# Latent attention on one core: rotary scores of the last three head pairs as two rounded passes over stacked query and residue, with the rotary projection copied to SBUF by ScalarE

## What is computed

```
q = (cq @ w_uq).reshape(B, S, 8, 128 + 64)
q_rope = apply_rope(q[..., 128:], cos, sin)
k_rope = apply_rope(d[..., 512:576], cos, sin)
s = (q_nope . k_nope + q_rope . k_rope) * sm_scale
p = softmax(where(key_pos <= q_pos, s, -inf))
o = p @ v
apply_rope: x1 * cos - x2 * sin, x2 * cos + x1 * sin
```

## Time and profile before

| | before |
|---|---|
| median of 3 runs (lowest, highest) | 1292.56 us (1291.3, 1292.88) |
| profiled execution, its time | 1291.86 us |
| profiled execution, its span | 1290.1 us |
| granted TensorE clock over the span | 0.999 |
| PE busy | 98% of the span |
| DVE busy | 72% |
| ACT busy | 47% |
| score steps of the latent attention | from 420.45 us to about 505.5 us |

### The profile page before, as it was taken

One profiled execution on the slowest core, in us unless ns is written; L12 is line 12 of the kernel. 1 busy time (PEld: TensorE's weight loads), 2 busy tenths in 40 slices (PEclk: granted clock), 3 DMA queues, 4 the chain that ended last, 5 costly groups with the idle time before them and its releaser, 6 DMA issues.

```text
span 1290.1 us, 19557 instructions
## 1 busy us (share of the span) xinstructions
PE 1268.9 (98%) x7451; PEld 1111.2 (86%) x7451; DVE 924.1 (72%) x1224; ACT 608.9 (47%) x888; POOL 31.4 (2%) x29
## 2 busy tenths in 40 slices
PE   8999999999999999999999999999999999999997
PEld 7799999988888777888999998888888878888887
DVE  6998787885447775678888787454768388887554
ACT  6444444554334555444444445334323255666444
POOL 0000000052000000000000000000000000000000
PEclk9999999999999999999999999999999999999999
DMA  5332433323332111232342433223625211113321
GB/s 195 104 93 68 129 95 101 114 90 103 96 102 80 43 50 66 66 98 67 98 124 71 130 90 114 90 89 106 184 66 164 66 53 46 49 50 131 99 66 66
DMA packets 159106, 119.69 MB, mean 93 GB/s; under 512 B 15228, under 2 KB 155976, under 8 KB 158792
## 3 DMA queue, kind: packets, MB, share of 16 engines
q1 hardware_dynamic: 158992, 118.89, 30.1%
q10 hardware_dynamic: 56, 0.01, 0.0%
HBM read 114.70 MB, written 4.19 MB: 92 GB/s over the span
## 4 chain that ended last, share of the span: by engine, by line
PE 75%; DVE 13%; issue 4%; ACT 4%; DMA 3%; SPq 1%; DVEq 0%; ACTq 0%
PE psum L2342 22%; PE psum L2344 21%; PE psum L2343 21%; DMA w_raw<-in_ffn_w_up 2%; PE psum L2570 1%; PE psum L2593 1%; DVE w_lo L1595 1%; PE psum L2755 1%; ACT w_hi L910 1%; ACT w_hi L804 1%; DVE w_lo L1407 1%; PE psum L2727 1%; PE psum L2739 1%; SPq L687 1%; DVE second_sum L1582 1%
## 5 line engine op out<-in xcount | busy, mean ns | idle before, releaser
L2342 PE MATMUL psum<-terms_hi,w_hi 128*128 128x256 f32 x1008 | 287.1, 285 | 2.9 <-ACT work L918 1.9
L2343 PE MATMUL psum<-terms_lo,w_hi 128*128 128x256 f32 x1008 | 285.2, 283 | 0.0
L2344 PE MATMUL psum<-terms_hi,w_lo 128*128 128x256 f32 x1008 | 285.1, 283 | 0.0
L2342 PE MATMUL psum<-xg_hi,w_hi 128*128 128x512 f32 x512 | 208.3, 407 | 1.6 <-ACT du L1255 0.9
L2344 PE MATMUL psum<-xg_hi,w_lo 128*128 128x512 f32 x512 | 199.8, 390 | 0.0
L2343 PE MATMUL psum<-xg_lo,w_hi 128*128 128x512 f32 x512 | 199.7, 390 | 0.0
L2342 PEld LDWEIGHTS psum<-terms_hi,w_hi 128*128 128x128 f32 x1008 | 193.3, 192 | 5.5 <-ACT work L918 3.7
L2343 PEld LDWEIGHTS psum<-terms_lo,w_hi 128*128 128x128 f32 x1008 | 193.4, 192 | 0.1
L2344 PEld LDWEIGHTS psum<-terms_hi,w_lo 128*128 128x128 f32 x1008 | 193.4, 192 | 0.0
L2342 PE MATMUL psum<-act_hi,w_hi 128*128 128x512 f32 x352 | 137.2, 390 | 0.0
L2344 PE MATMUL psum<-act_hi,w_lo 128*128 128x512 f32 x352 | 136.9, 389 | 0.0
(11 more groups left out here) (403 smaller groups left out, 2223.3 us busy)
## 6 DMA issues: line engine op xcount, KB each, us to landing
w_raw<-in_ffn_w_gate SPq DMA_DIRECT2D x72, 256.0 KB, 3.3
w_raw<-in_ffn_w_up SPq DMA_DIRECT2D x72, 256.0 KB, 3.7
w_raw<-in_w_in SPq DMA_DIRECT2D x16, 1024.0 KB, 5.3
w_raw<-in_ffn_w_down SPq DMA_DIRECT2D x16, 768.0 KB, 4.3
w_raw<-in_ffn_w_down SPq DMA_DIRECT2D x16, 640.0 KB, 4.1
w_raw<-in_ffn_w_gate SPq DMA_DIRECT2D x4, 1024.0 KB, 5.1
w_raw<-in_ffn_w_up SPq DMA_DIRECT2D x4, 1024.0 KB, 5.3
w_raw<-in_mla_w_o SPq DMA_DIRECT2D x4, 1024.0 KB, 5.0
```

The source lines that it names most:

```text
L2342: pe.matmul(o, wh, xh, start=start, stop=False, skip_group_check=True)
L2343: pe.matmul(o, wh, xl, start=False, stop=False, skip_group_check=True)
L2344: return pe.matmul(o, wl, xh, start=False, stop=stop, skip_group_check=True)
```

## The change

The first pair of heads keeps the product before. For pairs 1 to 3:

- ACT copies u from PSUM to `root` as soon as it is there. DVE multiplies it by the cosine on 128 partitions (`squares[:, 0]`), makes the crossed products with the sine in four pieces of 32 partitions (`rope_swap`, two pieces a call) and subtracts (`rope_sum`). ACT writes the rounded half of each head (two copies on 64 partitions, in `rope_tiles`), DVE the residue beside it on the other 64 partitions (`rope_lo`).
- `scores` takes the stacked query (rounded part and residue on 128 partitions) in two rounded passes, one with the rounded key on both halves (`kr_st[:, 0]`), one with the key's residue (`kr_st[:, 1]`). The key is split once: ACT at step 1, DVE at step 2.
- The product of the query's residue and the key's residue is now part of the sum as well; the float32 product is gone.
- u of pairs 2 and 3 is projected after the last step of the even head, one step earlier than before, and vb comes in its place. The split of the weights of pairs 2 and 3 is moved earlier: on ACT from steps 8 and 16 to steps 6 and 14, on DVE from steps 9 to 11 to steps 8 to 10 (17 to 19 to 16 to 18).

The diff, without the lists of semaphore marks:

```diff
--- before.py
+++ after.py
@@ -194,3 +194,4 @@
         kr = sb("kr", [P, T], stack=mla_mem)
-        q_rope = sb("q_rope", [P, 2, 2, T], stack=mla_mem)
+        q_rope = sb("q_rope", [P, 2, T], stack=mla_mem)
+        kr_st = sb("kr_st", [P, 2, T], F32R, mla_mem)
         cq_lo = sb("cq_lo", [P, 3, T], F32R, mla_mem)
@@ -257,3 +258,3 @@
 
-        QN, KN = 0, 2
+        QN, KN, QR = 0, 2, 4
 
@@ -442,3 +443,3 @@
         for pr in range(4):
-            used[FIRST["heads"] + pr] = (sem("proj_done"), 7 * pr + 7)
+            used[FIRST["heads"] + pr] = (sem("proj_done"), 7 * pr + 7 + (pr in (1, 2)))
             used[FIRST["mla_o"] + pr] = (sem("mla_o_done"), 2 * pr + 2)
@@ -462,6 +463,10 @@
                     return ((1, "u"),) if ii == 3 else ()
+                if ii == 3 and h + 2 < HEADS:
+                    return ((pr + 1, "u"),)
                 return ((pr, ("qn1", "kn1", "va", "vb")[ii]),)
+            if h + 1 == HEADS or ii == 3 or h == 1 and ii == 2:
+                return ()
             if h == 1:
-                return ((1, ("qn0", "kn0")[ii]),) if ii < 2 else ()
-            return ((pr + 1, ("u", "qn0", "kn0")[ii]),) if ii < 3 and h + 1 < HEADS else ()
+                return ((1, ("qn0", "kn0")[ii]),)
+            return ((pr, "vb") if ii == 0 else (pr + 1, ("qn0", "kn0")[ii - 1]),)
 
@@ -469,3 +474,3 @@
 
-        RESIDUED = [x for x in PROJ_ORDER if x[1][0] != "v"]
+        RESIDUED = [x for x in PROJ_ORDER if x[1][0] not in "uv"]
         VALUED = [x for x in PROJ_ORDER if x[1][0] == "v"]
@@ -486,4 +491,15 @@
 
+            if x[1] == "u":
+                return at(f"rope_kept{x[0]}") if x[0] else (sem("rope_turned"), 4)
             return (sem("values_kept"), VALUED.index(x) + 1) if x in VALUED else (sem("proj_ready"), RESIDUED.index(x) + 1)
 
+        def rope_pairs(s, later):
+
+            return [pr for pr in range(1, HEADS // 2) if s - later == NB * (2 * pr - 1) - 1]
+
+        def rope_tiles(pr, e):
+
+            x = xg_hi[:, QR + 2 * (pr % 2) + e, :]
+            return (x[64 * e:64 * e + 64, :], x[64 - 64 * e:128 - 64 * e, :], x)
+
         def proj_before(idx):
@@ -1050,2 +1066,7 @@
                     if what == "u":
+                        if pr:
+                            act.wait_ge(sem("proj_done"), idx + 1)
+                            if pr > 1:
+                                act.wait_ge(sem("rope_turned"), 8 * pr - 7)
+                            act.activation(root[:, :], proj_result(idx), ACT.Copy).then_inc(*mark(f"rope_kept{pr}"))
                         return
@@ -1103,2 +1124,6 @@
                     h, ii = divmod(s, NB)
+                    for pr in rope_pairs(s, 3):
+                        act.wait_ge(sem("rope_turned"), 8 * pr + 2)
+                        act.activation(rope_tiles(pr, 0)[0], squares[0:64, 0, :], ACT.Copy)
+                        act.activation(rope_tiles(pr, 1)[0], squares[64:128, 0, :], ACT.Copy).then_inc(*mark(f"rope_hi{pr}"))
                     if 0 < s <= NB * HEADS:
@@ -1112,4 +1137,9 @@
                         turned(s - 3)
-                    if h % 2 == 0 and ii == 0 and 0 < h < HEADS:
-                        split_hi(FIRST["heads"] + 1 + h // 2)
+                    if s == 1:
+                        act.activation(kr_st[0:64, 0, :], kr[0:64, :], ACT.Copy)
+                        act.activation(kr_st[64:128, 0, :], kr[0:64, :], ACT.Copy).then_inc(*mark("kr_st"))
+                    if h % 2 == 1 and ii == 2 and h + 3 < HEADS:
+                        split_hi(FIRST["heads"] + 1 + (h + 1) // 2)
+                    if s == NB * (HEADS - 2):
+                        split_hi(FIRST["mla_o"])
                     if s == NB * HEADS:
@@ -1807,2 +1837,19 @@
 
+                def rope_swap(pr, e):
+
+                    for r0, r1 in ((64 * e, 64 * e + 32), (64 * e + 32, 64 * e)):
+                        dve.tensor_tensor(squares[r0:r0 + 32, 1, :], root[r1:r1 + 32, :], sin_t[r1:r1 + 32, :], ALU.mult).then_inc(sem("rope_turned"), 1)
+
+                def rope_sum(pr):
+
+                    dve.wait_ge(sem("rope_turned"), 8 * pr + 1)
+                    dve.tensor_tensor(squares[:, 0, :], squares[:, 0, :], squares[:, 1, :], ALU.subtract).then_inc(sem("rope_turned"), 1)
+
+                def rope_lo(pr):
+
+                    dve.wait_ge(*at(f"rope_hi{pr}"))
+                    for e in range(2):
+                        hi, lo, _ = rope_tiles(pr, e)
+                        dve.tensor_tensor(lo, squares[64 * e:64 * e + 64, 0, :], hi.bitcast(F32), ALU.subtract).then_inc(sem("rope_turned"), 1)
+
                 def proj(pr, what):
@@ -1812,15 +1859,18 @@
                     done = sem("proj_ready")
-                    if idx:
-                        dve.wait_ge(done, RESIDUED.index((pr, what)))
                     if what == "u":
-                        dve.wait_ge(sem("proj_done"), idx + 1)
+                        dve.wait_ge(*(at(f"rope_kept{pr}") if pr else (sem("proj_done"), idx + 1)))
                         ps = proj_result(idx)
+                        if pr:
+                            dve.tensor_tensor(squares[:, 0, :], root[:, :], cos_t[:, :], ALU.mult).then_inc(sem("rope_turned"), 1)
+                            rope_swap(pr, 0)
+                            return
                         for e in range(2):
                             r = slice(64 * e, 64 * e + 64)
-                            dve.tensor_tensor(q_rope[0:64, pr % 2, e, :], ps[r, :], cos_t[r, :], ALU.mult).then_inc(sem("rope_turned"), 1)
-                            sine = dve.tensor_tensor(q_rope[64:128, pr % 2, e, :], ps[r, :], sin_t[r, :], ALU.mult)
-                            sine.then_inc(*((done, 1) if e else (sem("rope_turned"), 1)))
+                            dve.tensor_tensor(q_rope[0:64, e, :], ps[r, :], cos_t[r, :], ALU.mult).then_inc(sem("rope_turned"), 1)
+                            dve.tensor_tensor(q_rope[64:128, e, :], ps[r, :], sin_t[r, :], ALU.mult).then_inc(sem("rope_turned"), 1)
                         return
-                    hi = [x for x in RESIDUED if x[1] != "u"].index((pr, what)) + 1
-                    dve.wait_ge(sem("proj_hi"), hi)
+                    n = RESIDUED.index((pr, what))
+                    if n:
+                        dve.wait_ge(done, n)
+                    dve.wait_ge(sem("proj_hi"), n + 1)
                     dve.tensor_tensor(proj_tiles(idx, xg_lo), proj_result(idx), proj_tiles(idx, xg_hi).bitcast(F32), ALU.subtract).then_inc(done, 1)
@@ -1861,2 +1911,6 @@
                     h, ii = divmod(s, NB)
+                    for pr in rope_pairs(s, 1):
+                        proj(pr, "u")
+                    for pr in rope_pairs(s, 2):
+                        rope_swap(pr, 1)
                     if s < NB * HEADS:
@@ -1865,9 +1919,21 @@
                         for t in after_step(*divmod(s - 1, NB)):
-                            proj(*t)
+                            if t[1] != "u":
+                                proj(*t)
                     if s:
                         normalise(s - 1)
+                    for pr in rope_pairs(s, 2):
+                        rope_sum(pr)
+                    for pr in rope_pairs(s, 3):
+                        rope_lo(pr)
+                    if s == 2:
+                        dve.wait_ge(*at("kr_st"))
+                        for r in range(0, P, 64):
+                            low = dve.tensor_tensor(kr_st[r:r + 64, 1, :], kr[0:64, :], kr_st[0:64, 0, :].bitcast(F32), ALU.subtract)
+                        low.then_inc(*mark("kr_lo"))
                     if s - 1 in VALUE_STEPS and s % 2 == 0:
                         head_out(VALUE_STEPS[s - 1][0])
-                    if h % 2 == 0 and h and ii >= 1:
-                        split_lo(FIRST["heads"] + 1 + h // 2, ii - 1)
+                    if h % 2 == 0 and h and ii < 3 and h + 2 < HEADS:
+                        split_lo(FIRST["heads"] + 1 + h // 2, ii)
+                    if h == HEADS - 2 and ii >= 1:
+                        split_lo(FIRST["mla_o"], ii - 1)
                 split_lo(FIRST["mla_o"] + 1)
@@ -2563,4 +2629,6 @@
                         pe.wait_ge(sem("masks_ready"), 2)
-                    pe.wait_ge(sem("proj_ready"), proj_count(h // 2, f"kn{h % 2}", f"qn{h % 2}", "u"))
-                    pe.wait_ge(sem("rope_turned"), 3 * (h // 2) + 3)
+                    pe.wait_ge(sem("proj_ready"), proj_count(h // 2, f"kn{h % 2}", f"qn{h % 2}"))
+                    pe.wait_ge(sem("rope_turned"), 8 * (h // 2) + 4)
+                    if s == 2 * NB:
+                        pe.wait_ge(*at("kr_lo"))
                     if s >= 3:
@@ -2569,3 +2637,8 @@
                     triple(o, xg_hi[:, QN + hs, q], xg_lo[:, QN + hs, q], xg_hi[:, KN + hs, k], xg_lo[:, KN + hs, k], True, False)
-                    pe.matmul(o, q_rope[:, h // 2 % 2, hs, q], kr[:, k], start=False, stop=False, skip_group_check=True)
+                    if h < 2:
```

(5 more changed lines are left out.)

4 lines of the change are left out of this document (2 added, 2 removed).

## The result

| | before | after |
|---|---|---|
| median (lowest, highest), 4 runs each | 1292.16 us (1291.3, 1292.88) | 1305.86 us (1304.22, 1306.09) |
| ratio, 95% interval | | 1.0105 [1.0093, 1.0117] |
| span of the profiled execution | 1290.1 us | 1304.2 us |
| granted TensorE clock over the span | 0.999 | 0.992 |

The change costs 13.7 us. The direction was forecast, the size was not: 6.3 us were, and 1303.0 was the end of the range. The page's totals, against the earlier trace rows, hardly tell why: PE has a percent less of a longer span.

A forecast was written before the change was run, and what follows sets the result against it. PE was taken to bound inside a pair, DVE to be level at pair starts. 5.0 + 1.4 + 1.4 - 1.5 = +6.3 us on 1291.86, plus 0.7 for the median, gave 1298.9 us; range 1293.5 to 1303.0.

The forecast's parts named there:

- What bounds the kernel: Attention stage: PE is the bound inside a head pair; where a new pair begins, DVE is level with it.
- Part 1: Rotary score matmuls: two rounded passes replace the float32 product, saving 0.96 us a head, 5.8 us over six heads.
- Part 2: DVE per later pair: eight operations replace four multiplies, 0.72 us each; 2.9 us more per pair, 1.44 us more once.
- Part 3: ACT per later pair: one PSUM copy, 0.60 us, two rounded copies, 0.65 us each; fits idle time, not the order.
- Part 4: Way from u to a pair's first score: 5.0 us later at pair 1, 1.4 us each at pairs 2 and 3.
- rival 3: TensorE clock halves after each PE stall at the pairs' starts, say 1.5 us lost each time: 1303.4 us; chance 0.05.
- Rivals 1: Attention stage: PE stays the bound, new DVE and ACT work hides in their idle time: 1286.8 us; chance 0.12.
- 2: DVE operations on 32 partitions or in SBUF take about 0.45 us, making a draw: 1292.5 us; chance 0.08.
- 4: PE's two rounded passes cost the old 0.92 us: about 1302 us; chance counted inside the forecast's.

The follow-up runs named there:

- pe_only: The kernel before with the rotary product of heads 2 to 7 as two rounded passes, residues left out, DVE and ACT work unchanged: 1287.13 us.
- fill: The changed kernel with 18, 14 and 14 matmuls, whose results are overwritten, in PE's waits ahead of the later pairs' first scores: 1299.26 us.
- fp32_keep: The changed kernel with one float32 product of stacked query and rounded key in place of the two rounded passes: 1305.72 us.

## Why the prediction was wrong

- **What bounds the kernel.** Right: PE inside a pair, DVE level with it where a pair begins, and DVE's way once it grows. In pe_only, with PE's stream 1.54 us shorter, DVE's write is still what came last, 0.06 us ahead of the score.
- **Part 1.** Right, a little high: 0.52 us for two passes and mask, and 0.82 to 0.88 us a head where 0.96 was forecast.
- **Part 2.** Right: the spacing is 0.72 us for 32, 64 and 128 partitions, from SBUF or PSUM, so that the copy to SBUF made no product cheaper. Only the subtraction and the second residue have a spacing of 0.60.
- **Part 3.** Right: the two copies are in the sum and take 0.64 us each, and the split of the weights, for which 1.4 us were kept as a bound, cost nothing.
- **Part 4.** Right in mechanism and place, low in size. At full clock (fill) pair 1 is 5.35 us later (forecast 5.0), pairs 2 and 3 are 1.8 and 1.9 (1.4 each), the last stretch gives back 1.3 (1.5): 7.8 in the trace against 6.3. At pair 2 the excess builds up in small parts: in fill DVE's cosine starts 13.2 us after the first score of pair 1 (forecast 13.0), its residue of qn0 at 22.7 (22.3), the score at 26.4 (26.0). As time, fill has 6.7 over before, near the 6.3 of the forecast, which is thus the time of the changed kernel if the clock would hold.
- **The step that failed is the clock.** The forecast named waits of 3 to 5 us, counted nothing for the clock behind them, and left it to rival 3, with a chance of 0.05 and "say 1.5 us lost each time". "If each stall did this" was what the chip did, at all three places, and it cost 2.8, 1.6 and 1.6 us: the trace's 13.7 us are 6.3 forecast, 5.9 of clock and 1.5 of the way. The 1.5 us were no measurement. Rows for a low chance were thin: behind PE's first matmul the longest wait in the trace of before is 1.4 us (PE for ACT's work), so none shows a wait of 3 to 5 us inside the kernel. The one long stop, at its end, shows both sides: the clock held for 3.6 us after the last matmul and then fell to 0.51. The forecast's longest wait, 5 us at pair 1, was longer than that, and in the attention stage the clock fell sooner, 0.4 us into the wait at pair 1. The Trainium skill, TensorE: Matmul & The Clock Gate, Part 1, says that an idle PE falls back to 1.2 GHz; the runs agree, with 0.50 behind or in each wait of 2.93 us or more.
- **Rivals 1, 2 and 4** are out: PE stood 12 us at the three places, no rotary operation of DVE took 0.45 us, and the passes are cheaper. But in this order the cheaper pass gave nothing: fp32_keep is as fast as the change.
- **Slips in the sums**, none of which moves the result: u's time in Part 4 adds up to 12.3 us, not 12.4; 1.4 us later with 1.9 less to do is a stand of 3.3 us, not nearly 4; ACT's idle time a pair is 9 us by the earlier trace rows, not 8.

## What to carry to other kernels

Where a change lengthens the way to an engine's next work, count the wait, and then ask what the wait does to the clock behind it: here the second cost was 43% of the whole (5.9 of 13.7 us by the traces). Cheaper matmuls bring the next score nearer only if they lie ahead of the work that starts the way (here u); behind it they only make the wait longer. New work should be put where its result is due late (the odd head, four steps on), not where the whole pair waits for it; and an edit that fills a wait with useless matmuls tells in one run which share is clock.

## What was not expected of the hardware

- Equal waits of PE cost unequal time at half clock: 4.67 us was followed or overlapped by 10.2 us in two runs and by 6.8 in three; 2.70 and 2.78 us by 6.8 and by nothing. In after the clock fell 0.4 us into the wait at pair 1, but 0.7 us behind the end of that at pair 2. Why is left open.
- POOL's products between SBUF tiles held up DVE's small operations by up to 1.0 us each, 2.4 us for 5.84 us of POOL. POOL's product of 32 partitions takes 1.46 us here and 1.41 on average over the twelve, that of 64 partitions took 1.27 in before.
